# Where the inner activations of five FFNs begin in SBUF, modulo 512 bytes

## The reference

```python
def swiglu_ffn(x, w_gu, w_down):
    gate, up = jnp.split(x @ w_gu, 2, axis=-1)
    return (jax.nn.silu(gate) * up) @ w_down

x = x + 0.5 * swiglu_ffn(rms_norm(x, ffn1_norm[layer]), ffn1_w_gu[layer], ffn1_w_down[layer])
...
x = x + 0.5 * swiglu_ffn(rms_norm(x, ffn2_norm[layer]), ffn2_w_gu[layer], ffn2_w_down[layer])
...
f = (jax.nn.silu(h @ w_ffn_gate[l]) * (h @ w_ffn_up[l])) @ w_ffn_down[l]
```

## Time and profile before

| | |
|---|---|
| median of three runs | 3130.52 us |
| span of the profiled execution | 3127.9 us |
| TensorE matmul busy | 3112.8 us, 14504 records |
| TensorE weight load busy | 2517.6 us |
| VectorE busy | 1581.5 us |
| ScalarE busy | 1219.4 us |
| GpSimd busy | 318.7 us |
| HBM traffic | 92 GB/s over the span |

### The profile page before, as it was taken

The page is one execution under the profiler, slowest core; times in us unless marked ns, Lnnn a source line. Parts: engine busy times, 40 slices in busy tenths (PEclk is TensorE's granted clock), DMA queues, the critical chain, the costliest instruction groups (busy, mean ns, idle before and its releaser), DMA issues. The chain is left out here.

```text
span 3127.9 us, 37166 instructions
## 1 busy us (share of the span) xinstructions
PE 3112.8 (100%) x14504; PEld 2517.6 (80%) x14504; DVE 1581.5 (51%) x2479; ACT 1219.4 (39%) x1994; POOL 318.7 (10%) x454
## 2 busy tenths in 40 slices
PE   9999999999999999999999999999999999999999
PEld 8888886878888888888866878888887786788887
DVE  5443358754444344433566754443346876564433
ACT  4332247543232233223455543322335727443222
POOL 1000114211000000001210200000142200020000
PEclk9999999999999999999999999999999999999999
DMA  5333331412332333333222413332232231223332
GB/s 159 94 95 101 96 94 35 148 61 88 101 101 95 95 95 94 101 98 97 89 95 82 148 48 101 95 101 95 86 101 81 77 108 33 84 86 95 99 97 74
DMA packets 214368, 290.95 MB, mean 93 GB/s; under 512 B 13072, under 2 KB 138384, under 8 KB 214064
## 3 DMA queue, kind: packets, MB, share of 16 engines
q1 hardware_dynamic: 211120, 279.26, 28.6%
q0 software_dynamic: 2496, 8.98, 0.9%
q10 hardware_dynamic: 576, 0.33, 0.0%
HBM read 286.42 MB, written 2.10 MB: 92 GB/s over the span
## 5 line engine op out<-in xcount | busy, mean ns | idle before, releaser
L103 DVE TENSOR_TENSOR wl<-raw,wh 128x1024 fp32r<-128x1024 f32 (+2 forms) x531 | 654.1, 1239 | 1068.2 <-ACT wh L100 1064.3
L100 ACT ACTIVATE wh<-raw 128x1024 fp32r<-128x1024 f32 (+2 forms) x531 | 552.1, 1048 | 1142.9 <-PE ps L94 1103.8
L94 PE MATMUL ps<-hTh,wh 128*128 128x512 f32 x2400 | 942.1, 393 | 0.7 <-ACT hTh L100 0.7
L94 PE MATMUL ps<-hTh,wl 128*128 128x512 f32 x2400 | 938.0, 391 | 0.0
L94 PE MATMUL ps<-hTl,wh 128*128 128x512 f32 x2400 | 895.6, 391 | 0.2 <-DVE hTl L109 0.2
L94 PEld LDWEIGHTS ps<-hTh,wh 128*128 128x128 f32 x2400 | 450.8, 188 | 101.8 <-issue 9.9
L94 PEld LDWEIGHTS ps<-hTh,wl 128*128 128x128 f32 x2400 | 450.8, 188 | 97.3 <-issue 7.1
L94 PEld LDWEIGHTS ps<-hTl,wh 128*128 128x128 f32 x2400 | 449.4, 188 | 96.9 <-issue 4.7
L103 POOL TENSOR_TENSOR xn<-xn 128x512 f32<-128x512 f32 x69 | 99.2, 1438 | 1769.1 <-ACT xn L100 1531.7
L94 PE MATMUL ps<-wh,hTh 128*128 128x512 f32 (+2 forms) x576 | 216.8, 377 | 0.0
L94 PE MATMUL ps<-wl,hTh 128*128 128x512 f32 (+2 forms) x576 | 215.1, 374 | 0.0
(11 more groups left out here) (418 smaller groups left out, 4005.2 us busy)
## 6 DMA issues: line engine op xcount, KB each, us to landing
raw<-in_ffn_w_gu SPq DMA_DIRECT2D x350, 256.0 KB, 3.1
raw<-in_ffn_w_down SPq DMA_DIRECT2D x88, 512.0 KB, 3.5
raw<-in_xa_w_kv SPq DMA_DIRECT2D x32, 512.0 KB, 3.9
raw<-in_w_in SPq DMA_DIRECT2D x28, 512.0 KB, 3.7
raw<-in_od_w_in SPq DMA_DIRECT2D x24, 512.0 KB, 3.6
raw<-in_w_ffn_gate SPq DMA_DIRECT2D x44, 256.0 KB, 2.8
raw<-in_w_ffn_up SPq DMA_DIRECT2D x44, 256.0 KB, 3.1
raw<-in_w_ffn_down SPq DMA_DIRECT2D x22, 512.0 KB, 3.8
```

The costliest lines, as they stand in the source:

```text
L94: return self.made(lambda e: e.matmul(*a, **k))
L100: return self.made(lambda e: e.activation(*a, **k))
L103: return self.made(lambda e: e.tensor_tensor(*a, **k))
```

## The change

`Area.take` gets an argument `skew`, added after the step to 128 modulo 512. The class `Ffn` passes one for `Fh` and for `Fl`, another for each FFN: 96 (f10), 32 (f20), 64 (f11), 256 (f21) and 128 bytes (f3). `Fh` of f10 then begins at 126688 and `Fl` at 172256, both 224 modulo 512. The tiles behind them (`sg`, `pr`, `R`) are stepped to 128 modulo 512 as before and begin 1024 bytes higher. All other tiles, the instructions, their order and their waits stay as they are.

```diff
--- before.py
+++ after.py
@@ -156,10 +156,10 @@
     def __init__(self, at):
         self.at = at
 
-    def take(self, nc, name, shape, dt):
+    def take(self, nc, name, shape, dt, skew=0):
         n = 4 * int(np.prod(shape[1:]))
         if n % 512 == 0:
-            self.at = in_step(self.at)
+            self.at = in_step(self.at) + skew
         t = nc.alloc_sbuf_tensor_at(name, shape, dt, offset=self.at)
         self.at += -(-n // 32) * 32
         return t
@@ -1386,16 +1386,18 @@
 
 
     class Ffn:
-        def __init__(self, up, down, tag):
+        def __init__(self, up, down, tag, skew):
             area = Area(base)
             self.up, self.down = up, down
-            self.F = Act(sb(tag + "Fh", [P, KF, S], F32R, area), sb(tag + "Fl", [P, KF, S], F32R, area), S, ("F", up))
+            self.F = Act(area.take(nc, tag + "Fh", [P, KF, S], F32R, skew), area.take(nc, tag + "Fl", [P, KF, S], F32R, skew), S,
+                         ("F", up))
             self.sg = [sb(f"{tag}sg{i}", [P, S], F32, area) for i in range(2)]
             self.pr = [sb(f"{tag}pr{i}", [P, S], F32, area) for i in range(2)]
             self.R = sb(tag + "R", [P, S], F32, area)
 
-    ffns = {t: Ffn(u, d, t) for t, u, d in (("f10", "f1u0", "f1d0"), ("f20", "f2u0", "f2d0"), ("f11", "f1u1", "f1d1"),
-                                            ("f21", "f2u1", "f2d1"), ("f3", "f3u", "f3d"))}
+    ffns = {t: Ffn(u, d, t, k) for t, u, d, k in (("f10", "f1u0", "f1d0", 96), ("f20", "f2u0", "f2d0", 32),
+                                                  ("f11", "f1u1", "f1d1", 64), ("f21", "f2u1", "f2d1", 256),
+                                                  ("f3", "f3u", "f3d", 128))}
 
     def act_ffn_up(act, f):
         leave(act, f.up)
```

## The result

The changed kernel takes 3141.94 us (median of five runs, 3141.47 to 3143.70), the kernel before 3130.52 us in five runs beside them (3129.73 to 3130.95). The ratio is 1.0037 with a 95% interval from 1.0026 to 1.0048. That is 11.4 us slower and outside the 0.2% that I had called no change. The forecast of 3130.5 us was wrong; the time lies inside the range of 3112 to 3159.

A forecast was written before the change was run, and what follows sets the result against it. TensorE's chain of matmuls was taken to bound the kernel, busy 3112.8 of 3127.9 us. TensorE reads, VectorE/ScalarE accesses and DMA each counted 0, so the forecast stayed at 3130.5 us, range 3112 to 3159.

The forecast's parts named there:

- no change: Whole kernel: time within 6.3 us (0.2%) of before, the forecast case, chance 0.48.
- Reads by TensorE, the large term: Down stages: 2640 matmuls read F at moved addresses; bounded by 13.3 ns each either way, taken as 0.
- The upper bound: TensorE's reads of moved F: at most one more 32-cycle step, +13.3 ns per matmul.
- the sign of being wrong: Any of five down stages differing by over 2 us, or writes of F appearing among TensorE's waits.
- a further step per matmul: Slower rival, down stages: 13.3 ns more per matmul in f10, f20, f11; 21.1 us, 3151.6 us; chance 0.35.
- its second form: Further-step rival if any streamed-against-loaded skew counts: four FFNs pay 28.2 us (3158.7), with f3d 35.2 us (3165.7).
- The argument against it: Against the further step: 292 columns cost less excess, not more; 512 columns make 16 units, not 17.
- three totals: fp32r matmuls before: 544, 288 and 320 cycles for 512, 256 and 292 columns, read as whole multiples of 32.
- The gain: Faster rival, down stages: skew frees the excess; -21.1 us for f10, f20, f11, 3109.4 us; chance 0.15.
- The missing spread: Argument against the gain: f10Fh loads all last 187 to 188 ns, matmuls 389 to 390, so no giving way.
- The writes of F: VectorE and ScalarE writing skewed F: under 10 ns each, 0.4 us engine time per FFN, hidden, counted 0.
- the up stage: Stage before each down; rival that VectorE or ScalarE bounds it: 11 us for 0.2 us a group; chance 0.02.

The follow-up runs named there:

- the map: Changed kernel with other F skews, multiples of 32 bytes up to 480 over the five FFNs, three runs: 3144.91, 3145.05 and 3146.27 us against 3131.69.
- the kernel of matmuls alone: Separate kernel computing nothing of the reference: TensorE stretches of 48 matmuls at 64 differences, 0 to 252 bytes, plus full fp32, narrower loads, 256 columns; 2037.68 us.

## Why the prediction was wrong

**The step that failed** is "Reads by TensorE, the large term": "I take 0, by the rows nearest to it". Measured: +6.7 ns a matmul in f10 and f20, +2.2 in f11, 0 in f21 and +5.6 in f3d, so 528 x (6.7 + 6.7 + 2.2 + 0 + 5.6) = 11.2 us of the 11.8 by which the span grew. The upper bound, a step of 13.3 ns more, was sound: the worst difference found costs exactly that. The choice between them was not. I had argued that rows "in quite other parts of SBUF" have the same excess. But all those operands begin at 128 modulo 512, streamed and loaded: their difference was 0 in every row. Many rows with one value of the quantity in question say nothing on its effect. They should have left both ends of the bound with like chances, and the word "nearest" hid that. Three of the five stages moved by more than the 2 us that I had named as the sign of being wrong. That the time lies in the range is owed to the rival for which the range was drawn so wide, and not to the forecast.

**The rival** "a further step per matmul" had the right side and the right place, and it named the true condition among two ("or if stream and load must keep the same phase"). Its size was off: 16 cycles in f10 and f20 and not 32. So was its pattern: it let 128 bytes go free with 256, and it charged 64 as much as 96; in its second form, where any skew counts, it charged 256 too. The weights moved by 96 bytes show that at multiples of 32 bytes the phase between the two operands is what counts, and the map shows the period of 256 bytes.

**The argument against it** fell as well. That 292 columns cost less excess than 512 is no sign that addresses don't matter; the count of cycles moves in steps of another kind than I had read into three totals. The means of 560, 549.4 and 562.3 cycles could still be mixtures of multiples of 32, but in the kernel of matmuls alone the steps at the difference 104 are all 230 ns behind the first few, 552 cycles, which is none.

**The gain** did not come, at any of 64 differences: 226.7 ns was the least at 512 columns. The missing spread that I had held against it was a fact of the difference 0 alone: in f10 of the changed kernel the records last 392 to 402 ns. The Trainium skill (TensorE: Matmul & The Clock Gate, Back-to-back issue gap) has N/2.4 + 2.5 ns, 215.8 for 512 columns, which it calls the gap of an isolated matmul, and about 131 ns for a stream of loads and matmuls of 512 columns; I had taken the first for the rule of a stream. No fp32r stream of 512 columns in these runs went below 226.7 ns. The Trainium skill (SBUF — State Buffer, Specifications) has lines of 16 bytes, from which I had worked out a term of 0 for multiples of 32 bytes; the trace does not bear that out, 32 bytes cost 6.7 ns.

**What held:** 2640 matmuls in five stages are what is affected, each nanosecond of them comes through to the end, and nothing outside the down stages moved (the hTh and wh group is 942.7 us, against 942.1). The writes of F stayed at 633 and 691 ns, and the up stage never became late. Five different skews made the five stages differ, as I had said a price by residue would show.

**What stays open** is the mechanism. Loads a quarter as wide did not shrink the excess, so it is not the number of loaded columns. Steps depend on those before them, the sequences settle into short periods (231, 231, 238), and some differences have two steady states. What the two operands have in common is shown by no run; each of them loads anew for every matmul and goes round four PSUM banks. Why 512 columns take 544 cycles at best is open too.

## What to carry to other kernels

Keep the streamed and the loaded operand of every fp32r matmul at the same address modulo 256 bytes, both on a 32-byte boundary; 96 bytes in front of wl alone, with F of some FFNs moved too, cost 59.4 us in 3130, and 96 in front of wh and wl 73.7. When a change moves only addresses, ask which relation between operands the trace has never shown, and don't take many rows of one value for evidence. Where a program has like stages, give each another value: one profile then holds five answers.

## What the runs showed of the hardware

Distance of fp32r matmuls of 512 columns at the 2.4 GHz level, by where the streamed operand lies against the loaded one: 226.7 ns in step, 228.9 to 234.3 at the other multiples of 32 bytes, up to 240.0 at multiples of 4. At the multiples of 32 it repeats after 256 bytes. It is not symmetric (+4: 236.7, -4: 226.7). Off 32-byte boundaries an equal place does not free it (234.9 to 237.7 with both operands 4, 20, 196 or 244 bytes on), and twelve of 64 differences show two values by what ran before. TensorE alone shows it. Full fp32 doesn't have it, 429.2 ns for each of its records at all eight differences tried. At 256 columns in step is among the dearest: 120.0 ns in step and 120.1 at 96, but 117.8 at 32, 64 and 192 and 118.3 to 118.7 at 128, 160 and 224.
